# The latent attention's keys computed already turned, and its first heads' scores placed among the projections

## The reference

```python
q = (_rms_norm(h @ w_dq, q_norm) @ w_uq).reshape(bsz, s, 16, 64 + 32)
q_nope, q_rope = q[..., :64], _rotate(q[..., 64:], cos, sin)
kv_a = h @ w_dkv
c_kv = _rms_norm(kv_a[..., :256], kv_norm)
k_rope = _rotate(kv_a[..., 256:][:, :, None, :], cos, sin)[:, :, 0, :]
kv = (c_kv @ w_ukv).reshape(bsz, s, 16, 64 + 64)
k_nope, v = kv[..., :64], kv[..., 64:]
logits = q_nope . k_nope + q_rope . k_rope      # times 96 ** -0.5, causal mask
return softmax(logits) @ v, merged to 1024 columns, @ w_o
```

## Time and profile before

| what | us |
|---|---|
| median of 3 runs (range) | 1088.29 (1087.21 to 1093.13) |
| the profiled execution | 1089.14 |
| its span | 1087.3 |
| PE busy in the span | 1044.9 (96%) |
| DVE busy | 655.1 (60%) |
| ACT busy | 564.1 (52%) |
| POOL busy | 99.8 (9%) |

### The profile page before, as it was taken

One profiled execution on the slowest core, in us unless ns is written; L12 is line 12 of the kernel. 1 busy time (PEld: TensorE's weight loads), 2 busy tenths in 40 slices (PEclk: granted clock), 3 DMA queues, 4 the chain that ended last, 5 costly groups with the idle time before them and its releaser, 6 DMA issues.

```text
span 1087.3 us, 13860 instructions
## 1 busy us (share of the span) xinstructions
PE 1044.9 (96%) x5080; PEld 872.4 (80%) x5080; DVE 655.1 (60%) x1020; ACT 564.1 (52%) x855; POOL 99.8 (9%) x127
## 2 busy tenths in 40 slices
PE   7999999999999999999979999999997999999997
PEld 6887878887888887878867888888886878888886
DVE  5575665456565555647876755545654867555453
ACT  6566455437454455644544744454454647445541
POOL 2010110001000001104440100000140001000000
PEclk9999999999999999999989999999999999999999
DMA  8746136215545545633422655554252225555521
GB/s 336 279 174 230 58 117 219 110 58 183 204 159 190 215 149 187 237 136 118 152 75 103 234 188 196 188 192 153 70 190 105 78 92 221 191 195 190 193 78 39
DMA packets 28462, 176.31 MB, mean 162 GB/s; under 512 B 3248, under 2 KB 3392, under 8 KB 9984
## 3 DMA queue, kind: packets, MB, share of 16 engines
q1 hardware_dynamic: 26784, 170.08, 43.2%
q0 software_dynamic: 1456, 5.48, 1.4%
q10 hardware_dynamic: 176, 0.13, 0.0%
HBM read 174.62 MB, written 1.05 MB: 162 GB/s over the span
## 4 chain that ended last, share of the span: by engine, by line
PE 82%; DVE 9%; ACT 3%; issue 3%; POOL 2%; DMA 1%; SPq 0%; DVEq 0%; ACTq 0%; POOLq 0%
PE PS L1468 71%; PE PS L1537 3%; DVE w_lo L983 3%; PE PS L1589 2%; PE PS L1572 2%; ACT w_hi L572 2%; PE PS L1679 2%; DVE w_lo L981 1%; DMA x<-in_x 1%; DVE work L1127 1%; POOL h L487 1%; PE PS L1580 1%; DVE h L1347 1%; POOL arena L480 1%; ACT work L653 0%
## 5 line engine op out<-in xcount | busy, mean ns | idle before, releaser
L983 DVE SCALAR_TENSOR_TENSOR w_lo<-w_raw,gcol,w_hi 128x512 fp32r<-128x512 f32 (+4 forms) x322 | 269.4, 895 | 208.4 <-ACT w_hi L572 207.8
L572 ACT ACTIVATE w_hi<-w_raw,gcol 128x512 fp32r<-128x512 f32 (+4 forms) x322 | 243.4, 824 | 99.4 <-PE PS L1468 98.5
L1468 PE MATMUL PS<-w_hi,hT_hi 128*128 128x512 f32 (+3 forms) x904 | 246.4, 393 | 7.8 <-DVE hT_lo L998 3.0
L1468 PE MATMUL PS<-w_hi,hT_lo 128*128 128x512 f32 (+3 forms) x904 | 240.2, 386 | 0.0
L1468 PE MATMUL PS<-w_lo,hT_hi 128*128 128x512 f32 (+3 forms) x904 | 238.9, 385 | 0.9 <-DVE w_lo L983 0.8
L1468 PEld LDWEIGHTS PS<-w_lo,hT_hi 128*128 128x128 f32 x904 | 167.5, 188 | 35.9 <-DVE w_lo L983 2.4
L1468 PEld LDWEIGHTS PS<-w_hi,hT_hi 128*128 128x128 f32 x904 | 164.0, 189 | 40.1 <-issue 3.8
L1468 PEld LDWEIGHTS PS<-w_hi,hT_lo 128*128 128x128 f32 x904 | 168.1, 189 | 33.2
L981 DVE TENSOR_TENSOR w_lo<-w_raw,w_hi 128x2048 fp32r<-128x2048 f32 (+1 forms) x70 | 135.7, 1954 | 83.7 <-ACT w_hi L572 83.6
L572 ACT ACTIVATE w_hi<-w_raw 128x2048 fp32r<-128x2048 f32 (+1 forms) x70 | 114.6, 1644 | 106.7 <-PE PS L1468 106.7
L1468 PE MATMUL PS<-w_hi,gT_hi 128*128 128x512 f32 x408 | 113.9, 392 | 0.0
(11 more groups left out here) (151 smaller groups left out, 786.0 us busy)
## 6 DMA issues: line engine op xcount, KB each, us to landing
w_raw<-in_w SPq DMA_DIRECT2D x64, 1024.0 KB, 4.8
w_raw<-in_w_gu SPq DMA_DIRECT2D x22, 1024.0 KB, 4.8
w_raw<-in_w_in SPq DMA_DIRECT2D x11, 1024.0 KB, 7.6
w_raw<-in_w_dn SPq DMA_DIRECT2D x22, 512.0 KB, 5.4
w_raw<-in_w_mem_k SPq DMA_DIRECT2D x4, 1024.0 KB, 4.9
w_raw<-in_w_out SPq DMA_DIRECT2D x4, 1024.0 KB, 4.8
w_raw<-in_w_cq SPq DMA_DIRECT2D x4, 1024.0 KB, 4.7
w_raw<-in_w_mem_v SPq DMA_DIRECT2D x4, 1024.0 KB, 4.8
```

The lines of the kernel that those rows point to most:

```text
L572: ins = act.activation(w_hi[:, u % RING, k * w:(k + 1) * w], w_raw[:, u % RAW, k * w:(k + 1) * w], ACT.Copy, scale=1.0 if col is None else ...
L983: ins = dve.scalar_tensor_tensor(out=lo, in0=raw, scalar=gcol[:, col + TURNED * k:col + TURNED * k + 1], in1=hi, op0=ALU.mult, op1=ALU.sub ...
L1468: mm = pe.matmul(bank(t, j)[:, 0:width], rows[:, kc0 + k, tok], w[:, s, at:at + width], start=begin and i == 0, stop=end and i == 2)
```

## The change

It does five things.

1. Keys. The weight unit of keys and values is split head by head into a key half and a value half (`by_head`, `by_part`). `keys(g)` then takes the weights as the stationary side and the turned latents as the moving side, so that the keys come out already turned, two heads in 128 PSUM rows and 256 tokens. Four copies of 64 rows (two on ScalarE, two on VectorE) bring them to `kT4`. The values are made apart, in the old orientation (`values_of`). The turns of the keys go. Since the tokens are no longer on the rows, the norm's factor is multiplied in earlier, when the latents are copied to `d_tok`.
2. The shared rotated part is turned once (two turns of 96 columns in the bank of the last latents), VectorE copies it to head 0's rows 64 to 96 of `kT4`, and GpSimd copies it to the other 15 heads (`spread_rope`, 32 partitions by 3840 values).
3. The latents of the queries and of the keys are turned and split apart, and the queries' of tile 1 go ahead of the last unit of the projection's tile 0.
4. The queries are rotated tile by tile.
5. The scores of heads 0, 1 and 2 stand between the last products of keys and values on TensorE, and both first units of the output projection are split before head 0 and no longer between the heads.

```diff
+        def by_head(cols):
+            heads = cols.rearrange("p (h s d) -> p h s d", s=2, d=64)
+            return [heads[:, :, s, :] for s in range(2)]
+        def by_part(cols):
+            return [cols[:, 512 * s:512 * s + 512].rearrange("p (h d) -> p h d", d=64) for s in range(2)]
+        def key_places(g, b):
+            first = 8 * g + 4 * b
+            return [(kT4[LOW, first + i:first + 4:2, :], PS[64 * i:64 * i + 64, b, :].rearrange("p (h m) -> p h m", m=SEQ)) for i in range(2)]
...
+            def spread_rope():
+                tb_done(pool, KEY_BANK)
+                pool.tensor_copy(kT4[64:96, 1:16, :], kT4[64:96, 0:1, :].to_broadcast([32, 15, SEQ])).then_inc(rope_spread, 1)
...
+                    raw, hi = (tile[:, u % RING, k * w:(k + 1) * w] for tile in (w_raw, w_hi))
+                    for source, high in zip(by_head(raw), by_part(hi)) if FIRST["ukv"] <= u < FIRST["odd_out"] else [(raw, hi)]:
+                        ins = act.activation(high, source, ACT.Copy, scale=1.0 if col is None else gcol[:, col + TURNED * k:col + TURNED * k + 1])
...
+            split_to(e + 1)
+            high_queries(0)
+            high_keys(0)
+            split_to(e + 2)
+            square_latents(1)
+            split_to(e + 3)
+            high_queries(1)
...
+            evict(0, queries(0), query_rows)
+            split_to(e + 5)
+            evict(1, queries(0), query_rows)
+            high_keys(1)
+            split_to(e + 6)
+            n["used"] += 3
+            evict(0, queries(1), query_rows)
+            act.wait_ge(padded, 6)
+            plain_banks(4, heads96(qT4, 0))
+            split_to(e + 7)
+            evict(1, queries(1), query_rows)
+            n["used"] += 2
+            copy_keys(0)
+            split_to(e + 8)
+            plain_banks(4, heads96(qT4, 1))
+            copy_values(0)
+            split_to(e + 9)
+            attention(mla, [0])
+            copy_keys(1)
+            attention(mla, [1])
+            copy_values(1)
...
+            def copy_latents(t):
+                s, key = rows_stat(4, t), LATENTS + 2 * t + 1
+                dve.wait_ge(ss_ready, LATENTS + 2 * t + 1)
+                dve.tensor_copy(d_tok[:, t, 0:384], PS[:, 2 * t, 0:384]).then_inc(latent_ready, 1)
+                dve.wait_ge(rstd_ready, key + 1)
+                dve.tensor_scalar(d_tok[:, t, 384:640], PS[:, 2 * t + 1, 0:256], rstd[:, key:key + 1], None, ALU.mult)
                 dve.tensor_scalar(d_tok[:, t, 640:672], PS[:, 2 * t + 1, 256:288], rstd[:, s:s + 1], None, ALU.mult)\
                     .then_inc(acc_copied, 1)
...
+            def rotate_queries(g, t):
+                dve.wait_ge(acc_copied, n["copied"] - 1 + t)
+                rotate(heads_of(stages[g][:, t:t + 1, :], 96), 64, 16, cos4[:, t:t + 1, :], sin4[:, t:t + 1, :], 512 * t).then_inc(h_ready, 1)
+            def copy_keys(g):
+                dve.wait_ge(keys_done, 2 * g + 2)
+                for place, bank in key_places(g, 1):
+                    ins = dve.tensor_copy(place, bank)
+                ins.then_inc(keys_copied, 1)
+            def copy_values(g):
...
+            copy_latents(0)
+            split_to(e + 1)
+            low_queries(0)
+            low_keys(0)
+            split_to(e + 2)
+            copy_latents(1)
+            low_queries(1)
...
-            steps.link(dve.tensor_copy(k_rope, d_tok[:, :, 640:672]))
+            rotate(heads_of(d_tok[:, :, 640:672], 32), 0, 16, cos4, sin4, 1024).then_inc(rope_ready, 1)
+            n["copied"] += TT
+            split_to(e + 4)
+            rotate_queries(0, 0)
+            split_to(e + 5)
+            rotate_queries(0, 1)
...
+            dve.tensor_copy(kT4[64:96, 0, :], PS[64:96, 4 + n["tb"] % 4, 2 * P:4 * P])
+            low_keys(1)
+            split_to(e + 6)
...
-            attention(mla, rows=h)
+            plain_banks(4, heads96(qT4, 0))
+            rotate_queries(1, 0)
+            rotate_queries(1, 1)
+            split_to(e + 7)
+            n["used"] += 8
+            copy_keys(0)
+            plain_banks(4, heads96(qT4, 1))
+            split_to(e + 8)
+            copy_values(0)
+            split_to(e + 9)
+            attention(mla, [0])
+            copy_keys(1)
+            attention(mla, [1])
+            copy_values(1)
+            attention(mla, range(2, mla.H + 2), False, h)
...
             def turn_latents(t):
                 pe.wait_ge(acc_copied, n["down"] + 1 + t)
-                turn([d_tok[:, t, P * b:P * (b + 1)] for b in range(4)])
-                turn([d_tok[:, t, 4 * P:5 * P]])
+                latent = [d_tok[:, t, P * b:P * (b + 1)] for b in range(3, 5)]
+                if t == 0:
+                    turn(latent)
+                    return
+                assert n["tb"] == KEY_BANK
+                pe.wait_ge(rope_ready, 1)
+                bank = 4 + n["tb"] % 4
+                for i in range(TT):
+                    pe.transpose(PS[0:96, bank, (2 + i) * P:(3 + i) * P], d_tok[:, i, 576:672], ident[:])
+                turn(latent)
...
+            def keys(g):
+                u = n["u"]
+                high_ready(u)
+                for bank in range(2):
+                    for p in range(2):
+                        pair = 2 * bank + p
+                        for i in range(3):
+                            if i == 2:
+                                split_ready(u)
+                            for k in range(2):
+                                rows, w = three(u % RING, k, slice(P * pair, P * (pair + 1)), None)[i]
+                                mm = pe.matmul(PS[:, bank, p * SEQ:(p + 1) * SEQ], w, rows, start=i == 0 and k == 0, stop=i == 2 and k == 1)
+                    mm.then_inc(keys_done, 1)
+            def values_of(g):
+                u = n["u"]
+                for t in range(TT):
+                    for i in range(3):
+                        for k in range(2):
+                            rows, w = three(u % RING, k, slice(512, 1024), t)[i]
+                            mm = pe.matmul(PS[:, 2 + t, :], rows, w, start=i == 0 and k == 0, stop=i == 2 and k == 1)
+                    mm.then_inc(values_done if t == 0 else w_used, 1)
+                n["u"] += 1
...
+            project(4, 2, [384, 288], copies=2, rows=rows, hooks={(0, 3): tile1, (1, 3): first_latents})
             latents = n["tb"] - 2
-            project(3, 1, [384, 384], copies=2, rows=latents, hooks={(1, 0): lambda: turn_latents(1)})
-            project(3, 1, [384, 384], copies=2, hooks={(1, 1): after_h(lambda: turn_heads(0))})
-            project(1, 2, wide, kc0=3, copies=2, rows=latents, hooks={(1, 0): after_h(lambda: turn_heads(1), 2)})
-            project(1, 2, wide, kc0=3, copies=2, hooks={(1, 0): lambda: turn_keys(0)})
-            wait_h()
-            turn_keys(1)
-            turned(4)
-            attention(mla, rows=h)
+            project(3, 1, [384, 384], copies=2, rows=latents, hooks={(0, 2): lambda: turn_queries(1)})
+            project(3, 1, [384, 384], copies=2, hooks={(0, 0): lambda: turn_latents(1), (1, 0): after_h(lambda: turn_heads(0), 2)})
+            tb_done(pe, latents + 1)
+            tb_done(pe, latents + 3)
+            pe.wait_ge(acc_copied, n["copied"] - 1)
+            keys(0)
+            wait_h(2)
+            turn_heads(1)
+            copied()
+            values_of(0)
+            pe.wait_ge(keys_copied, 2)
+            pe.wait_ge(rope_spread, 1)
+            turned(8)
+            attention(mla, [0])
+            keys(1)
+            attention(mla, [1])
+            pe.wait_ge(values_copied, 2)
+            values_of(1)
+            attention(mla, [2])
+            pe.wait_ge(keys_copied, 4)
+            pe.wait_ge(values_copied, 4)
+            attention(mla, range(3, mla.H + 3), h)
```

More of the change, by code:

```diff
@@ L944, in query_rows @@
             def query_rows(t):
                 return LATENTS + 2 * t
-            def key_rows(t):
-                return LATENTS + 2 * t + 1
-            group(3, queries(0), query_rows, ahead=2)
-            group(3, queries(1), query_rows, lambda: plain_banks(4, heads96(qT4, 0)), 1)
-            group(1, keys(0), key_rows, lambda: plain_banks(4, heads96(qT4, 1)), 0)
-            group(1, keys(1), key_rows, lambda: plain_banks(4, heads96(kT4, 0)), -1)
-            plain_banks(4, heads96(kT4, 1))
@@ L981, in split @@
                         ins = dve.tensor_tensor(lo, raw, hi, ALU.subtract)
+                    elif FIRST["ukv"] <= u < FIRST["odd_out"]:
+                        for low, source, high in zip(by_part(lo), by_head(raw), by_part(hi)):
+                            ins = dve.scalar_tensor_tensor(out=low, in0=source, scalar=gcol[:, col + TURNED * k:col + TURNED * k + 1],
+                                                           in1=high, op0=ALU.mult, op1=ALU.subtract)
                     else:
```

98 lines of the change are left out of this document (49 added, 49 removed).

## The result

The changed kernel takes 1078.1 us (median of 4 runs, 1076.7 to 1079.3), the kernel before beside it 1090.6 (1087.2 to 1093.1). The ratio is 0.9891, with a 95% interval of 0.9872 to 0.9910: some 12 us faster. The profiled execution took 1079.18 us (span 1077.4).

A forecast was written before the change was run, and what follows sets the result against it. TensorE, busy 96%, bounds the kernel; in the changed stage VectorE's list ends last, so the output projection starts at 861.5 instead of 873.44: 1089.14 - 12.0 = 1077.1 us, range 1072.8 to 1082.2.

The forecast's parts named there:

- The stage: TensorE from first product of the queries to first of the output projection: 63.4 us instead of 75.3.
- The start of tile 1: TensorE's query products of tile 1, after VectorE's key latents copy and split: taken at 802.8, between 801.6 and 804.2.
- VectorE's list as the last one: From 810.35, 19.7 us of work plus 3.4 for GpSimd's copy, ending at 833.45, last of all ahead of head 3.
- GpSimd's copy: Copy of 3840 values beside VectorE's four-piece split: taken at 3.4 us, whole length counted into VectorE's list.
- The sign named for it: In the profile after, one of VectorE's four pieces behind GpSimd's copy is longer by that copy.
- TensorE's waits: Idle 1.3 us at 815.1, 1.7 at 818.8, 0.8 at 825, 1.3 at 833.8; nothing counted for the clock.
- TensorE's own list: TensorE's work ahead of head 3's scores: 15.6 us from 814.5, so 830.1, 5 us ahead of 835.1.
- A: Rival: GpSimd's copy runs beside VectorE, nothing blocks; gain 15.4 us, time 1073.7; chance 0.20.
- B: Rival: GpSimd's copy takes 7.1 us and blocks; gain 8.3, time 1080.8, up to 1082.2 with the clock; chance 0.15.
- C: Rival: GpSimd's copy far slower than any row, everything waits; at 6 ns a value 1096.7 us; chance 0.04.
- D: Rival: unseen waits in the new order give the gain back, to under 5.4 us; chance 0.06.
- the two weight units between the heads: Heads 3 to 15: 22.8 us where 12 heads at 1.66 us need 19.9, thus 2.9 us lost.

The follow-up runs named there:

- taking it away in two ways: Changed kernel with the rotated part spread by ScalarE instead of GpSimd: 1074.5 us; or by a transfer from SBUF to SBUF instead: 1074.4 us.
- the run with two copies: Changed kernel with GpSimd's copy of the rotated part made twice, one behind the other: 1080.4 us, ratio 0.9924 to the kernel before.
- the last experiment: Kernel with two copies moved, but rotated part spread by a transfer and all four copies of second turned queries on ScalarE: 1072.8 us, ratio 0.9845.
- the transfer: Changed kernel with the rotated part spread to heads 1 to 15 by an SBUF-to-SBUF transfer instead of GpSimd's copy: 1074.4 us, ratio 0.9874.
- two copies moved: Kernel where ScalarE spreads, plus ScalarE makes VectorE's copy of first values and copies second values ahead of head 1's exponentials: 1072.6 us, ratio 0.9856.

## Why the prediction was right

- **The stage** was forecast at 63.4 us and took 63.34; everything outside was forecast unchanged, and the 213.9 us behind it are. The start isn't: it came 2.06 us late, which puts the profiled execution at 1079.18 us against 1077.1.
- **The start of tile 1**, an estimate of 4.7 us behind the first product, was 4.59 (804.76 - 800.17).
- **VectorE's list as the last one** holds. It was forecast to end at 35.34 us behind the stage's start and ended at 835.47 - 800.17 = 35.30; head 3's scores, forecast at 37.04, stood at 37.04. The agreement to 0.1 us is partly luck, since it is better than the terms: the four pieces with the copy were put at 6.05 and took 5.79 (to 818.35), the two rotations at 2.8 and took 2.65 (819.55 to 822.20), the start of the pieces was at 12.39 instead of 12.24, and each pair of key copies took 1.4 instead of 1.25. The errors are small, of both signs, and cancel.
- **GpSimd's copy** took 3.76 us, above the 3.4 taken and far below 7.1, 0.98 ns a value. What it costs VectorE is 3.13 us, below 3.4, as one copy and two copies show alike. That it must be charged to VectorE, the step on which most hung, is shown by taking it away in two ways. The sign named for it is there too: one of the four pieces is longer by 3.14 us and the others are not. The Trainium skill, "GPSIMD Engine Reference", section 1, has such a contention for instructions with two SBUF inputs; the trace agrees for the split, and the page gives no price.
- **TensorE's waits** ahead of head 3 were put at 1.3, 1.7, 0.8 and 1.3 us and were 1.12, 1.20, 0.65 and 1.34. No clock fell in the stage (granted 1.00). The argument for it was weak, though: it took waits shorter than the 3.3 us of the earlier trace rows for harmless, and in the last section the clock falls behind waits of 1.46 and 1.74 us. The forecast was safe by its other half, that a fall would hide in TensorE's lead, as the run with two copies shows.
- **TensorE's own list** was put at 32.0 us behind the start, 5 us ahead of head 3. In the last experiment head 3's scores stood at 32.82 with a wait of 0.58, so 32.2. A 256-column product took 0.12 us (24 of them by two in 0.24 us), as taken.
- **The rivals.** A would have been a stage of 60 us or less: without the exclusion it was 60.93 and 60.79, so its size was a little too good: with the transfer VectorE waits 0.47 us for ScalarE at the rotation, and its two pairs of key copies take 0.3 us more than forecast. The exclusion that it denied is real. B's copy of 7.1 us didn't come; doubling the copy to 7.5 us gave 66.47, near B's 75.3 - 8.3 = 67.0, with the fall of the clock that B expected and none of its price. C and D find nothing in the trace: no wait of TensorE in the stage is longer than 1.34 us.

One term of the forecast isn't worth the same everywhere. It put the two weight units between the heads at 2.9 us. On the kernel before, by itself, moving them gives 2.75. In the changed kernel the same placement is worth 1.4 only, since it saves 2.92 us behind head 3 and makes head 3 itself 1.50 us later.

## What to carry to other kernels

A copy put on an idle engine isn't free if it reads and writes SBUF beside VectorE's two-input instructions (here 3.13 of 3.76 us came back on VectorE): count GpSimd's length into VectorE's list, or give the copy to ScalarE in a stretch where it waits, or to a transfer. When one engine's list is without gaps, add it up from the first instruction to the last; but check each instruction that another engine must answer before the list goes on, since the delay of such a loop isn't covered by the other's lead elsewhere. A lead counts only the waits behind the place that is delayed. And once the longest list is cut, the next one is only a few us behind: here 3.9 us of cutting brought TensorE's own work to the front.

## What the hardware showed that I had not expected

The same wait doesn't always bring the clock down. Early in the program, in code that the change doesn't touch, TensorE waits 1.07 and 1.46 us in short succession, in every kernel of this study. In before (first fence) the products behind it ran at full speed; in the changed kernel's execution (second) they didn't:

```profile
138.14 1.17 PE L1468 MATMUL PS<-w_hi,hT_hi 128*128 128x512 f32 x4 [1.46 <-issue]
```
```profile
138.95 2.04 PE L1560 MATMUL PS<-w_hi,hT_hi 128*128 128x512 f32 x4 [1.46 <-issue]
```

The windows from 135 to 145 us of before and of the changed kernel say the same (the third number from the end is the granted clock):

```profile
135.00:145.00 10.00, 7.49 (x34) 6.13 (x35) 2.79 (x6) 2.24 (x4) 0.00 (x0) 1.00 0.04 16
```
```profile
135.00:145.00 10.00, 7.47 (x30) 5.75 (x29) 3.60 (x9) 1.60 (x3) 0.00 (x0) 0.83 0.12 51
```

Of the ten profiled executions of this study two have this fall, the changed kernel's and that with two copies moved (2.05 us for the same row), and the eight others have 1.15 to 1.17. It costs some 1.4 us (the two groups of products from 138.95 to 142.30 take 3.35 us, before from 138.14 to 140.07 1.93), and is most of the 2.06 us by which the changed kernel's stage began late; some 0.8 us were there before it (136.86 against 136.05), and where they are from isn't shown.

Two more executions, the kernel before with its units early and the changed one with the transfer, have a fall elsewhere: behind a wait of 1.73 and 1.74 us at 109 that all ten have, the scores of a head take 1.59 us instead of 0.87, here with the transfer:

```profile
111.06 1.59 PE L1664 MATMUL PS<-arena 128*128 128x128 f32 x4
```

So four of ten executions have one of these two falls, none has both, and six have neither. A difference of one execution in code that wasn't changed is no effect of the change: I took stage against stage, and the medians of the runs for the whole.
